# Low-rank decay products between the q and the k projection of the first mixer, and a tile of the mixers 64 bytes further on

## What is computed

```
q, k, v, a_low, r, q_mem = jnp.split(h @ gla_w_in[j], GLA_SPLITS, axis=-1)
log_a = jax.nn.log_sigmoid(a_low @ gla_w_alpha[j] + gla_b_alpha[j]) / GLA_GATE_TAU
o = gla_attention(q, k, v, log_a)
o = rmsnorm(o, gla_out_norm[j]) * jax.nn.silu(r)
o_mem = memory_cross_attention(q_mem, rmsnorm(mem, mem_norm[i]), ...)
x = x + jnp.concatenate([o, o_mem], axis=-1) @ w_out[i]
```

## Time and profile before

| | |
|---|---|
| median of 3 runs | 2106.94 us (2106.02 to 2107.75) |
| the profiled execution | 2105.29 us |
| its span | 2103.5 us |
| mean granted clock of TensorE | 0.928 |
| TensorE matmul busy | 1826.4 us (87%) |
| DVE busy | 810.4 us (39%) |
| ACT busy | 598.8 us (28%) |
| moved by DMA | 603.69 MB, mean 287 GB/s |

### The profile page before, as it was taken

One profiled execution on the slowest core, in us unless ns is written; L12 is line 12 of the kernel. 1 busy time (PEld: TensorE's weight loads), 2 busy tenths in 40 slices (PEclk: granted clock), 3 DMA queues, 4 the chain that ended last, 5 costly groups with the idle time before them and its releaser, 6 DMA issues.

```text
span 2103.5 us, 30749 instructions
## 1 busy us (share of the span) xinstructions
PE 1826.4 (87%) x13288; PEld 1356.2 (64%) x13288; DVE 810.4 (39%) x947; ACT 598.8 (28%) x706; POOL 132.0 (6%) x141
## 2 busy tenths in 40 slices
PE   9999999999999999999999996676677667677666
PEld 8999997999999997599999731222222212222221
DVE  7655557865665564766658500000000000000000
ACT  6333546533433354654327300000000000000001
POOL 4200011400000000220001000000000000000000
PEclk9999999999999999999999988788778888788888
DMA  8555452555555454156556999999999999999998
GB/s 272 180 179 169 156 187 95 180 182 189 189 192 192 155 184 129 39 194 218 179 182 237 410 427 429 427 428 428 428 428 428 428 428 428 428 429 428 429 429 339
DMA packets 182536, 603.69 MB, mean 287 GB/s; under 512 B 11952, under 2 KB 139440, under 8 KB 158016
## 3 DMA queue, kind: packets, MB, share of 16 engines
q1 hardware_dynamic: 180560, 601.43, 73.6%
q10 hardware_dynamic: 1648, 0.70, 0.1%
q0 software_dynamic: 256, 0.52, 0.1%
HBM read 601.58 MB, written 1.05 MB: 286 GB/s over the span
## 4 chain that ended last, share of the span: by engine, by line
PE 57%; DMA 40%; DVE 2%; ACT 1%; issue 0%; SPq 0%; ACTq 0%; POOL 0%; DVEq 0%; POOLq 0%
PE ps L1079 22%; DMA bulk<-in_w_up 19%; PE ps L1093 12%; DMA bulk<-in_w_down 10%; DMA bulk<-in_w_gate 10%; PE ps L1256 3%; PE ps L1669 2%; PE ps L1150 2%; PE ps L1045 2%; PE ps L1149 2%; PE ps L1151 2%; PE ps L1159 1%; PE ps L1161 1%; PE ps L1160 1%; PE ps L1279 1%; PE ps L1133 1%
## 5 line engine op out<-in xcount | busy, mean ns | idle before, releaser
L1079 PE MATMUL ps<-part,part 128*128 128x256 f32 x3840 | 460.1, 280 | 0.1
L1079 PEld LDWEIGHTS ps<-part,part 128*128 128x128 f32 x3840 | 455.5, 188 | 0.5 <-DVE part L2268 0.3
L1669 PE MATMUL ps<-bulk 128*32 128x512 f32 x1616 | 249.3, 748 | 150.9 <-DMA bulk<-in_w_up 91.6
L2268 DVE TENSOR_TENSOR part<-bulk,part 128x2048 fp32r<-128x2048 f32 x88 | 202.8, 2346 | 220.0 <-ACT part L1763 220.0
L1669 PEld LDWEIGHTS ps<-bulk 128*32 128x32 f32 x1616 | 50.2, 123 | 333.0 <-issue 129.8
L1093 PE MATMUL ps<-part,part 128*128 128x256 f32 x2112 | 255.5, 280 | 0.0
L1093 PEld LDWEIGHTS ps<-part,part 128*128 128x128 f32 x2112 | 251.8, 188 | 0.0
L1763 ACT ACTIVATE part<-bulk 128x2048 fp32r<-128x2048 f32 x86 | 160.1, 1910 | 227.0 <-DMA bulk<-in_ffn_w_up 227.0
L2903 DVE TENSOR_TENSOR keep<-keep,ps 128x512 f32<-128x512 f32 x16 | 11.0, 687 | 530.0 <-PE ps L1669 530.0
L1697 PE MATMUL ps<-bulk,keep 128*32 128x512 f32 x784 | 113.1, 713 | 30.0 <-DMA bulk<-in_w_down 29.4
L2277 DVE TENSOR_TENSOR part<-bulk,part 128x2048 fp32r<-128x2048 f32 x45 | 103.1, 2305 | 46.6 <-ACT part L1778 46.5
(11 more groups left out here) (327 smaller groups left out, 2227.1 us busy)
## 6 DMA issues: line engine op xcount, KB each, us to landing
bulk<-in_w_gate SPq DMA_DIRECT2D x53, 2048.0 KB, 40.7
bulk<-in_w_up SPq DMA_DIRECT2D x48, 2048.0 KB, 40.0
bulk<-in_w_down SPq DMA_DIRECT2D x48, 2048.0 KB, 40.2
bulk<-in_ffn_w_gate SPq DMA_DIRECT2D x44, 1024.0 KB, 5.5
bulk<-in_ffn_w_up SPq DMA_DIRECT2D x44, 1024.0 KB, 8.0
bulk<-in_ffn_w_down SPq DMA_DIRECT2D x44, 1024.0 KB, 5.3
keep<-in_w_up SPq DMA_DIRECT2D x16, 2048.0 KB, 41.0
keep<-in_w_down SPq DMA_DIRECT2D x15, 2048.0 KB, 40.7
```

The costliest lines, as they stand in the source:

```text
L1079: ins = pe.matmul(y, w_, x_, start=(k == m == 0), stop=(k == KD - 1 and m == 2))
L1669: ins = pe.matmul(ps[j * CAP:(j + 1) * CAP, half, :], xe[:, k, :], w[:, kk, j * HALF:(j + 1) * HALF], start=(k == 0), stop=(k == KD - 1))
L2268: dve.tensor_tensor(hi(slot(3 * b + i)), slot(3 * b + i), as32(w_hi(f, b, i)), ALU.subtract).then_inc(gu_split, 1)
```

## The change

On TensorE the low-rank product `al` is issued between q3 and k0 instead of behind k3. Its evacuation on ACT moves to the end of the q part too. In the table `al` takes the fifth place (g = 4), so k0 to k3 get g = 5 to 8: k1 and k3 are evacuated by ACT now, k0 and k2 by DVE, where it was the other way round; `al` stays with ACT, and the `la` tiles keep engine and bank. `catT_hi` begins at word 3088 instead of 3072.

```diff
--- before.py
+++ after.py
@@ -426,7 +426,7 @@
 
         plan_mem(0)
         g = 0
-        for nm in [f"q{h}" for h in range(GH)] + [f"k{h}" for h in range(GH)] + ["al"] + [f"la{h}" for h in range(GH)]:
+        for nm in [f"q{h}" for h in range(GH)] + ["al"] + [f"k{h}" for h in range(GH)] + [f"la{h}" for h in range(GH)]:
             plan(nm, g % 8, alt[g % 2])
             g += 1
         for nm in [f"{w}{s}{t}" for w in "vr" for s in range(4) for t in range(TT)] + [f"qm0.{h}" for h in range(EH)]:
@@ -661,7 +661,7 @@
 
 
         catT = v3(0, CAT, T)
-        catT_hi = v3(3072, CAT, T)
+        catT_hi = v3(3088, CAT, T)
         memH = v3(15376, KD, T)
         mk = v3(3072, EH, T)
         mv = v3(4096, TT, MEMW)
@@ -1297,11 +1297,13 @@
 
             mem_kv(0, 1)
             fed(1, 3)
-            for w, c0 in (("q", 0), ("k", 512)):
+            def queries_or_keys(w, c0):
                 for h in range(GH):
                     wt = weights(("gla", c0 + (h // 2) * CW))
                     begin(f"{w}{h}")
                     end(turned_split(f"{w}{h}", wt, (h % 2) * P, XNT))
+
+            queries_or_keys("q", 0)
             begin("al")
             pe.wait_ge(alow_split, 1)
             for k in range(KD):
@@ -1309,6 +1311,7 @@
                     ins = pe.matmul(tbank("al")[0:GRANK, 0:T], hi(w_)[:, k, :], hi(x_)[:, k, :], start=(k == m == 0),
                                     stop=(k == KD - 1 and m == 2))
             end(ins)
+            queries_or_keys("k", 512)
             pe.wait_ge(alpha_loaded, 16)
             pe.wait_ge(*out_of("al"))
             for h in range(GH):
@@ -1959,8 +1962,9 @@
                     if h % 2 == 0:
                         split_ahead(("gla", c0 + (h // 2) * CW))
                     evac(f"{w}{h}", dst[:, h, :])
+                if w == "q":
+                    evac("al", al_T[0:GRANK, :], tbank("al")[0:GRANK, 0:T])
             split_ahead(("gla", 1024))
-            evac("al", al_T[0:GRANK, :], tbank("al")[0:GRANK, 0:T])
             for h in range(GH):
                 evac(f"la{h}", gt1[:, h, :], func=ACT.Identity, bias=vcol("gla_b", h))
             for h in range(GH):
```

## The result

The changed kernel takes **2109.77 us** (median of 22 runs, 2108.28 to 2112.18), the kernel before, on the same chip, 2106.00 (22 runs). The ratio is 1.0018, interval 1.0012 to 1.0023: 3.8 us slower, where 3.24 was forecast. The profiled execution has a span of 2108.6 us at a mean granted clock of 0.923; before it was 2103.5 and 0.928.

A forecast was written before the change was run, and what follows sets the result against it. Bound by TensorE getting its operands up to about 1200 us, then by streaming expert weights. Later r tile 2.04 + low clock 1.6 - catT_hi 0.4 = +3.24 us on 2106.94 gives 2110.2 us, range 2105.8 to 2112.4.

The forecast's parts named there:

- main case: Whole kernel: stall at the first r tile plus low clock behind it, 2110.2 us, given 47%.
- Step 1: TensorE, al ahead of k: k runs 2.80 us later, the 0.51 us wait goes, la starts at about 251.76.
- Step 2: TensorE behind la: clock stays up, saving 1.6 us; TensorE reaches the r tile at 276.5, 2.3 us earlier.
- Step 3: ACT/DVE chain: uncovered split of tile 1536 delays it 2.71 us; TensorE idles 4.3, r tile 2.04 us later.
- Step 4: TensorE behind the stall at the r tile: one low-clock stretch costing 1.6 us, bounds 0 and 3.2.
- Rival B: First r tile: the stall comes without a low clock behind it, 2108.6 us; chance 18%.
- Step 5: L1256 products: moving catT_hi 16 words frees four slow weight tiles and slows two quick ones, -0.4 us.
- theory of like offsets: L1256: weights and activations at like offsets cost 2.2 ns a product.
- Rival A: ACT/DVE chain has slack, so the stall and its low clock are void: 2104.3 us; chance 10%.
- Rival D: DVE or ACT regains half of the chain's 2.7 us delay: 2107 us; chance 5%.
- Rival C: The 16-column al block between q and k brings the low clock: 1.6 us more, 2111.8 us; chance 20%.

The follow-up runs named there:

- e2_tile: The kernel before with catT_hi at word 3088 alone, al still behind k: 2105.81 us, ratio 1.0001.
- e8_early_old: The kernel before, al behind k, with the first r tile's weight split (ACT copy, DVE subtraction) and DVE's v00 evacuation made early: 2106.06 us, ratio 0.9997.
- e3_dve: The changed kernel with DVE's two la evacuations ahead of its split of tile 1536: 2105.49 us, ratio 0.9999 to the kernel before.
- e4_fill: The changed kernel with 30 full-size products, results overwritten, filling TensorE's wait before the first r tile: 2107.86 us, ratio 1.0012 to the kernel before.
- e5_al2: The changed kernel with the 24 al products done twice: 2112.90 us, ratio 1.0030 to the kernel before.
- e7_both: The changed kernel with catT moved to word 16 as well: 2108.57 us, ratio 1.0010 to the kernel before.
- e1_order: The changed kernel with catT_hi back at word 3072, the move of al alone: 2109.81 us, ratio 1.0020 to the kernel before.
- e9_best: The changed kernel with e3_dve's order, first r tile's split and v00 evacuation made early, catT at word 16: 2102.31 us, ratio 0.9985 to the kernel before.

## Why the prediction was right, and where it was off

Sign, mechanism and time came out as forecast, the main case within 0.2%: 2110.2 said, 2109.8 measured. That the two are so close is partly luck. The kernel before, run beside the change, took 2106.00 us and not the 2106.94 that I added to, so the change itself cost 3.8 where I had 3.24. And the terms of the 3.24 missed both ways: by the rows the stall was 0.3 too high, the low clock 1.0 too low, and a gain of 0.4 did not come.

**Step 1** held. The wait is gone; `la` is 25.54 us behind q, before 26.10, so 0.56 sooner.

**Step 2** had the outcome and not the cause. The clock is 1.00 behind `la` in the change. But it is so too in e2_tile and e8_early_old, which have the old order with its wait. So the old order doesn't always bring the fall in the earlier trace rows; the profiled execution that I counted from happened to have it. None of the eleven profiled executions with the new order has it, against one in three with the old, which is too few to say that the order prevents it. It changed the sum little, because the chain takes back most of it: with the clock up (e2_tile) A is 51.75, with it down 52.42.

**Step 3** is confirmed by e3_dve: the cover that goes is the one named, and the stall falls with the place of DVE's evacuations. Sizes: 2.43 us on the chain where I had 2.71, mostly because DVE's two evacuations take 0.87 us and not 1.10. I had taken a merged row in which the second may have waited for its `la` tile (in e3_dve they come 0.86 us apart). TensorE's idle time came to 3.62 us, not 4.3: 0.3 of the difference is the chain, and the rest is that TensorE got there later than my 276.5. TensorE's r tile comes 1.76 us later than in the profiled execution (2.04 said), and 2.43 later than in an old-order execution with the clock up. One stall, not several, is right too.

**Step 4** was mis-sized: 1.6 us forecast. Against the 67.23 of e4_fill, B says 2.52 in the change, 2.55 in e5_al2, 2.34 in e7_both and 1.52 in e1_order. I took the price of another low stretch for this one; one execution in four has that price, the others lie midway between it and my bound of two stretches, 3.2. That the low stretch comes from the gap is shown by e4_fill, where the filled gap leaves none. **Rival B**, the stall without a low clock, falls by this.

**Step 5** was wrong in size. -0.4 forecast, 0.0 measured (34.57 and 34.58 us; e2_tile's ratio 1.0001). The step that failed is "moving catT_hi should free the four slow tiles": it brought them from 120.0 to 118.9 ns, half of the way, and the two quick tiles lost all they had. `catT`, which every third product reads, had stayed where it was; that this is why only half came is not shown, since e7_both refutes the theory of like offsets behind the term. By the Trainium skill, SBUF — State Buffer, section Who interferes with whom, the term was 0, and so it came out, but the weight tiles differ by up to 7 ns a product, which that section doesn't explain.

The sum by the rows: stall 1.76, low clock 2.63, tile 0, together 4.39 against 3.24 (2.52 of the 2.63 by e4_fill, the other 0.11 is in e2_tile's and e3_dve's B too and has no cause here). The medians say 3.8. **Rival A**, that the chain has slack, fell with the 3.62 us wait. **Rival D**, that half of the 2.7 us comes back, fell with the 2.43 that arrived. **Rival C**, the low clock in the `al` products, fell with the clock of 1.00 from the first q product to the stall in the change, and by e5_al2.

## What to carry to other kernels

When work is moved off an engine's busy stretch, ask what it was covering on the other engines: here 2.8 us of small products hid a weight split, and taking out a 0.5 us wait cost 3.8. Then look at the lists of those engines for a long operation that itself waits, in front of a short one that heads a chain; changing the two round cost nothing and gave 4.3 us back. And price a stall of TensorE as the delay plus the slow products behind it: here 2.4 us of delay, counted from the old order with the clock up (e2_tile), became 3.9 to 5.0 in the rows of e1_order and the change.

## What the hardware showed that was not expected

- The same 3.62 us gap in front of the same products left the granted clock at 0.50 until before 285 in one execution (e1_order) and until nearly 287 in another (the change), 1.0 us of time apart. In the first it fell behind the gap (0.68 from 281 to 282), in the second inside it (0.53 from 280 to 281). Gaps of 0.67 and 1.18 us left it at 1.00.
- The spacing of equal products of 256 columns depends on where their operands start: 120.0, 118.9, 117.8, 116.7 and 113.3 ns a product at the same line, by shifts of 32 to 128 bytes. It doesn't depend on the activations' places alone, as the two mixers differ (e9_best). The Trainium skill, SBUF — State Buffer, section Operand start alignment, treats start addresses as a matter of legality and says that its runs timed nothing; its TensorE: Matmul & The Clock Gate, section Back-to-back issue gap, has a formula for the isolated gap at the full clock, which gives an estimate of 109.2 ns for 256 columns. The quickest tiles come within 4 ns of it, the others don't. What in the memory makes the difference no run here shows.
